# Expert weight blocks of a mixture-of-experts layer, each loaded by two half transfers

## The reference

```python
def swiglu(h, w_gate, w_up, w_down):
    return (jax.nn.silu(h @ w_gate) * (h @ w_up)) @ w_down

def moe_swiglu(h, w_router, b_router, w_gate, w_up, w_down):
    logits = (h @ w_router).astype(jnp.float32) + b_router.astype(jnp.float32)
    top_v, top_i = lax.top_k(logits, TOP_K)
    ...
    for e in range(N_EXPERTS):
        out = out + gates[..., e:e + 1] * swiglu(h, w_gate[e], w_up[e], w_down[e])
    return out
```

## Time and profile before

| | us |
|---|---|
| median of 3 runs | 1657.58 (1657.5 to 1658.97) |
| the profiled execution, its own time | 1659.68 |
| its span, first to last instruction | 1657.9 |

### The profile page before, as it was taken

How to read it: one execution, slowest core, us unless ns; L and a number is a source line. 1 busy time by engine, 2 the same in 40 slices (tenths; PEclk the granted TensorE clock), 3 DMA queues, 4 the chain that set the end, 5 groups by cost and what they waited for, 6 DMA issues and landing times.

```text
span 1657.9 us, 26870 instructions
## 1 busy us (share of the span) xinstructions
PE 1580.1 (95%) x11274; PEld 962.1 (58%) x11274; DVE 769.3 (46%) x1771; ACT 375.0 (23%) x841; POOL 80.6 (5%) x156
## 2 busy tenths in 40 slices
PE   6999999989999999999898999899999999999997
PEld 3655456878888888884775555333343443334343
DVE  5987983578868857877688270000010001000101
ACT  4333543321101110016665422100000000000002
POOL 2210100000000021000103100000000000000000
PEclk9999999999999999999999999999999999999999
DMA  8503553233635635112244389999999999999995
GB/s 322 168 9 120 210 148 102 75 114 117 203 108 146 203 96 108 51 52 102 65 169 90 110 339 396 413 413 407 408 412 415 403 405 411 415 408 406 411 412 203
DMA packets 170840, 396.42 MB, mean 239 GB/s; under 512 B 34499, under 2 KB 93483, under 8 KB 153562
## 3 DMA queue, kind: packets, MB, share of 16 engines
q1 hardware_dynamic: 165344, 391.23, 63.7%
q0 software_dynamic: 4112, 3.34, 1.3%
q10 hardware_dynamic: 1258, 0.07, 0.0%
HBM read 389.36 MB, written 1.05 MB: 235 GB/s over the span
## 4 chain that ended last, share of the span: by engine, by line
PE 85%; DMA 8%; ACT 3%; DVE 2%; issue 1%; SPq 1%; ACTq 0%; DVEq 0%
PE ps L1369 82%; DMA arena<-in_moe_w_up_dram 6%; PE ps L1372 3%; DMA norms<-in_moe_w_gate_dram 1%; DMA arena<-in_moe_w_gate_dram 1%; SPq L712 1%; ACT work L873 0%; ACT work L872 0%; ACT dg L881 0%; ACT work L1124 0%; DVE norms L2585 0%; ACT arena L1034 0%; DVE work L2592 0%; ACT arena L1141 0%; ACT hT L832 0%
## 5 line engine op out<-in xcount | busy, mean ns | idle before, releaser
L1369 PE MATMUL ps<-arena,work 128*32 128x256 f32 (+6 forms) x4588 | 608.0, 480 | 14.9 <-DMA arena<-in_moe_w_up_dram 9.0
L1369 PEld LDWEIGHTS ps<-arena,work 128*32 128x32 f32 (+2 forms) x4588 | 271.8, 125 | 320.5 <-issue 249.5
L1369 PE MATMUL ps<-arena 128*128 128x256 f32 (+2 forms) x1152 | 288.4, 478 | 6.2 <-ACT arena L1034 5.2
L3274 DVE TENSOR_TENSOR work<-work,ps 128x768 f32<-128x768 f32 (+4 forms) x26 | 18.6, 727 | 513.1 <-PE ps L1369 513.1
L1369 PEld LDWEIGHTS ps<-arena 128*128 128x128 f32 (+1 forms) x1152 | 186.4, 185 | 95.4 <-issue 67.6
L1369 PE MATMUL ps<-work 128*64 128x64 f32 (+11 forms) x2300 | 224.5, 329 | 14.0 <-DVE work L3007 6.7
L1369 PEld LDWEIGHTS ps<-work 128*64 128x64 f32 (+5 forms) x2300 | 158.1, 154 | 73.1 <-issue 55.7
L1369 PE MATMUL ps<-work,arena 128*128 128x256 f32 (+1 forms) x588 | 126.5, 368 | 0.0
L1289 ACT ACTIVATE work<-ps 128x512 f32<-128x512 f32 (+3 forms) x35 | 17.7, 505 | 445.7 <-PE ps L1372 445.7
L1369 PEld LDWEIGHTS ps<-work,arena 128*128 128x128 f32 (+1 forms) x588 | 103.2, 190 | 13.3
L1369 PE MATMUL ps<-apad,dg 64*64 64x512 f32 (+1 forms) x384 | 67.5, 490 | 9.2 <-ACT dg L881 5.9
(11 more groups left out here) (446 smaller groups left out, 1466.3 us busy)
## 6 DMA issues: line engine op xcount, KB each, us to landing
arena<-in_moe_w_down_dram SPq DMA_DIRECT2D x66, 1024.0 KB, 17.2
arena<-in_moe_w_up_dram SPq DMA_DIRECT2D x54, 1024.0 KB, 18.2
arena<-in_w_ada_dram SPq DMA_DIRECT2D x23, 2048.0 KB
arena<-in_moe_w_gate_dram SPq DMA_DIRECT2D x46, 1024.0 KB, 16.6
arena<-in_moe_w_up_dram SPq DMA_DIRECT2D x26, 768.0 KB, 16.8
arena<-in_moe_w_gate_dram SPq DMA_DIRECT2D x22, 768.0 KB, 15.9
norms<-in_moe_w_down_dram SPq DMA_DIRECT2D x13, 1024.0 KB, 15.9
arena<-in_w_in_dram SPq DMA_DIRECT2D x6, 2048.0 KB
```

Of the source, the lines that this page charges most:

```text
L1369: return pe.matmul(o, lhs, rhs, start=start, stop=stop)
L3274: last = tt_(o, o, ps[rows, 2:4, :].rearrange("p b n -> p (b n)")[:, at_:at_ + n], ALU.mult)
```

## The change

Every expert block is sent as two transfers, both onto the block's semaphore. The tiny expert's gate and up blocks are cut by columns, 2 x 1408; all others by rows, [128, 1, w] each. TensorE waits for both: `landed_at` counts 32 per block. Order, places, and what SP waits for ahead of a block stay.

```diff
         def landed_at(n):
-            return 16 * (n // NSEM + 1)
+            return 2 * 16 * (n // NSEM + 1)
...
-                    sp.dma_start(wblock(n)[:, :, 0:src.shape[-1]], src.rearrange(order, p=P)).then_inc(block_in(n), 16)
+                    w = src.shape[-1]
+                    to, rows = wblock(n)[:, :, 0:w], src.rearrange(order, p=P)
+                    for half in range(2):
+                        if w == FE:
+                            part = (slice(0, 1), slice(FE // 2 * half, FE // 2 * half + FE // 2))
+                        else:
+                            part = (slice(half, half + 1), slice(0, w))
+                        sp.dma_start(to[:, part[0], part[1]], rows[:, part[0], part[1]]).then_inc(block_in(n), 16)
```

## The result

The changed kernel takes 1663.07 us in the median of 8 runs (1661.18 to 1663.33), the kernel before 1657.62 us beside it. The ratio is 1.0027, 95% interval 1.0017 to 1.0037, so the change costs 4.5 us, between 2.8 and 6.1. Timed once more with more runs of the kernel before (changed_again), the ratio is 1.0030 (1.0018 to 1.0043): 5.0 us. Slower was forecast, by 6.4 us, and the time lies 0.9 us under the forecast of 1664.0.

The account below looks back on a forecast made before the run. The full DMA stream was taken to bound the kernel through the 231st block; 4.6 us of data packets plus 2.0 of semaphore packets, 6.6, on the median 1657.58 gave 1664.2, forecast as 1664.0; likeliest case 1661 to 1668, whole range 1658.0 to 1672.

Parts of the forecast that it names:

- The bound: Last 700 us: the DMA engines never pause from 1040 to 1620 us, and their stream sets when PE can finish.
- The deciding block: The 231st expert transfer, landing at 1538.18 us, which PE waits for; from 1538.32 on PE's work runs to the end.
- PE's long stretch: 1188 to 1520 us, PE busy 332.00 of 332 us; claimed to be slack for the change.
- SP's issues: 272 more transfers issued on SP, some 0.8 us per block instead of 0.4; cost nothing, hidden under the stream.
- Data packets, 4.6 us: Ahead of the 231st block, 8576 more data packets at 8.56 ns over 16 engines: 4.6 us, lower bound 3.8.
- Semaphore packets, 2.0 us: Ahead of the 231st block, 3696 more semaphore packets at 8.56 ns: 2.0 us, bounds 0 and 6.9 us.
- After the deciding block: Last 41 blocks: 3088 more packets, 1.7 us, hidden in PE's 6.0 us of slack at the last block.
- Nothing to be seen: Rival: 8 KB stretches are fast because their bytes neighbour in HBM; only 2.0 us remain, 1659.6; chance 0.20.
- a price per transfer: Rival: each transfer's fixed part isn't wholly hidden; 11.5 us at the 30 ns bound, 1669.1; chance 0.14.
- all exposed: Rival: every transfer's fixed part shows, 2.4 us each for 231 transfers, 560 us, some 2200; chance 0.01.
- Faster: Rival: packets follow closer when engines take row 0 of all partitions, then row 1; 1649.4 at 5 ns; chance 0.13.
- What the profile should show: Some 186200 packets, 6270 of 8 KB and more, full stretches 402 to 410 GB/s, late transfer about 7 us later.

Follow-up runs that it names:

- split_long: Kernel before with only the 70 paired down blocks (row halves) and 16 tiny-expert blocks (column halves) cut in two: 1.0031, +5.1 us.
- one_transfer_unpaired: Kernel before, one transfer per block, but every down block takes its two rows 128 apart, so 8 KB packets become 4 KB: 1.0022, +3.6 us.
- column_halves: Kernel before with all 272 blocks sent as two transfers of half the columns each: 1.0216, +35.8 us.
- longer_packets: Kernel before with wide and narrow gate and up blocks read as 128 rows of twice the columns, one transfer each: 0.9978, -3.6 us.
- sp_padding_12: Kernel before with twelve already satisfied semaphore waits on SP ahead of each expert transfer: 1.0014, +2.3 us.
- quarters: Kernel before with every block in four transfers (half a row pair by half the columns), the tiny expert's in two: 1.0250, +41.4 us.
- split_short: Kernel before with only the 186 blocks whose packets are not shortened (wide, narrow, unpaired down) sent as row halves: 1.0001, +0.2 us.
- tail_halves: Kernel before with the change for the last 41 blocks only, the first 231 whole: 1.0002, +0.3 us.

## Why the prediction was right, and where it was off

*The bound.* Right. The deciding block is the one that was named, in the changed kernel, in split_long and in one_transfer_unpaired, and it lands later by what the stream has lost. In column_halves it is the same block and then one more in the tail, for 2.0 us. (PE's row has one 8 among the 9s that the prediction reads there, in the 26th slice; nothing hangs on it.) That PE's long stretch is slack for a slower stream, and the bound for a faster one, is shown by longer_packets.

*SP's issues.* Right that they cost nothing by their time. An unblocked one still takes 0.33 us at the least. The median landing in 1060 to 1188 us went from 18.6 to 14.0 us: fewer bytes stand in the queue ahead of a transfer, with no effect, as the DMA share stays at 1.03. What wasn't in the sum is SP's code: six more instruction packets, about 1 us if the price of sp_padding_12 holds for them, which no run shows.

*Data packets, 4.6 us.* Right in mechanism, and in size as far as the runs can tell. one_transfer_unpaired (3.6 for 3.5), split_long (5.1 for 4.6) and the late block of column_halves (33.2 for 34.0) measure it three times; the landings of this block in the profiles, 3.7 us apart, are somewhat under it.

*Semaphore packets, 2.0 us.* Off; this is the term of the sum that was mis-sized. I gave them the fixed price of any packet. They are free in full stretches, by quarters against column_halves (2939 more of them and no byte less), and split_short, with 1.4 us of them by that price, costs 0.2 (-1.3 to 1.5), which agrees but doesn't decide. Without that term, and with r and c solved from data packets alone (2230 and 1422 in the stretches from 1500 and 1600 us), r is 26.98 bytes/ns and c 8.72 ns. The sum is then 8576 x 8.72 / 16 = 4.7 us, against 4.5 and 5.0 measured. With about 1 us of code it would be 5.7, so the change itself gives no sign that the code term is needed.

*After the deciding block.* Right: hidden, by the chains of the changed kernel and of tail_halves.

*Rivals.* "Nothing to be seen" falls with split_long and one_transfer_unpaired, "a price per transfer" with split_short and with column_halves, "all exposed" with the DMA share. "Faster" would have needed packets that follow closer in the new order; split_short has that order in 186 blocks and gains nothing. The advice of the Trainium skill ("DMA: Bandwidth & Descriptors", Rules for kernel authors) of at least 1 MiB per transfer did not bear on this stream: with several transfers in flight, split_short sends most of it in 384 and 512 KB pieces at no measurable cost. The fixed 2.0 us that the prediction takes from the Trainium skill (same page, Anatomy of one DMA) is its figure for transfers issued by GpSimd; these are issued by SP, and the rival's price was worked out from the 5.0 us in the earlier trace rows.

*What the profile should show.* Packets, those of 8 KB, no stretch at 415 GB/s, and the late block's place all came out. It was to land about 7 us later and landed 3.0 and 3.7 us later in the two profiles; some of this is the scatter of single executions, some the 2.0 us that don't exist. The last block was to land 8 us later and landed 4.5 to 5.6 us later.

## What to carry to other kernels

In a stream that keeps the DMA engines full, count packets, not transfers: a packet is one run of bytes that are contiguous on both sides, and each data packet cost about 8.6 ns of one engine beyond its bytes here, 5% of its time at 4 KB and 3% at 8 KB. Cut a transfer where no run is cut, and not into halves of 64 partitions (17% of the time here), and expect nothing from it if the consumer waits for both halves. Where two resources are both full, find the one place where the one has caught up with the other: a loss ahead of it counts whole, a gain only as far as there is a wait to shorten.

## What was not expected of the hardware

* A transfer to 64 partitions in a queue of such transfers moves 235 to 237 GB/s, one to 128 partitions with 4 KB packets 403 to 410, both at a DMA share of 1.02 to 1.03. The Trainium skill ("SBUF — State Buffer", Door 1: The DMA port swizzle) says that partitions 0 to 63 reach 8 of 16 ports, with some 218 GB/s at best, and (same page, Can I just issue two DMAs to hit both halves?) that two such transfers can't be combined. The trace agrees in kind, with 8% more.
* Semaphore packets are free in a full stream (5878 against 2939 in 240 us, 92.36 against 92.33 MB).
* Instructions that SP runs without any transfer can slow a kernel with a full stream: 3264 waits that never waited cost 2.3 us (0.8 to 4.0). Why is not shown.
